# First gate and up blocks of the second feed-forward layer in alternating fours of halves, with all of x for them turned by VectorE

## The reference

```python
x = x + 0.5 * swiglu(rms_norm(x, n1), g1, u1, d1)          # D_FF = 5632
x = x + head_group_mixer(rms_norm(x, n2), w_in, ..., w_out) # 16 attention heads, 4 retention heads
x = x + 0.5 * swiglu(rms_norm(x, n3), g2, u2, d2)          # the layer that is changed
y = rms_norm(x, final)
def swiglu(h, w_gate, w_up, w_down):
    return (silu(h @ w_gate) * (h @ w_up)) @ w_down
```

## Time and profile before

| what | value |
|---|---|
| median of three runs | 1797.8 us (1797.42 to 1798.38) |
| the profiled execution, its own time | 1797.76 us |
| its span | 1795.9 us |
| TensorE matmul busy | 1786.4 us, 99% |
| VectorE busy | 1271.0 us, 71% |
| ScalarE busy | 811.8 us, 45% |
| mean granted TensorE clock | 0.999 of full |

### The profile page before, as it was taken

The page is one execution under the profiler, slowest core; times in us unless marked ns, Lnnn a source line. Parts: engine busy times, 40 slices in busy tenths (PEclk is TensorE's granted clock), DMA queues, the critical chain, the costliest instruction groups (busy, mean ns, idle before and its releaser), DMA issues.

```text
span 1795.9 us, 22263 instructions
## 1 busy us (share of the span) xinstructions
PE 1786.4 (99%) x8104; PEld 1476.3 (82%) x8104; DVE 1271.0 (71%) x1622; ACT 811.8 (45%) x976; POOL 59.2 (3%) x57
## 2 busy tenths in 40 slices
PE   9999999999999999999999999999999999999998
PEld 7888888888888888888888888888888888888886
DVE  6676676676676678688888786676676667667668
ACT  6434444444443444555455445443443443444444
POOL 0000000000000000002222000000000000000000
PEclk9999999999999999999999999999999999999999
DMA  9655565565555555555546456556556556655552
GB/s 382 206 187 190 198 195 187 190 199 195 187 191 199 193 187 193 182 168 190 183 163 211 141 181 217 193 199 193 187 192 200 192 187 192 200 192 187 193 200 97
DMA packets 175590, 346.66 MB, mean 193 GB/s; under 512 B 5952, under 2 KB 8640, under 8 KB 175424
## 3 DMA queue, kind: packets, MB, share of 16 engines
q1 hardware_dynamic: 174976, 345.35, 57.8%
q10 hardware_dynamic: 576, 0.81, 0.1%
HBM read 344.04 MB, written 2.10 MB: 193 GB/s over the span
## 4 chain that ended last, share of the span: by engine, by line
PE 98%; DMA 0%; ACT 0%; issue 0%; DVE 0%; SPq 0%; POOLq 0%; POOL 0%; DVEq 0%; ACTq 0%
PE ps L381 32%; PE ps L382 32%; PE ps L383 32%; PE ps L410 0%; DMA raw<-in_g 0%; PE ps L598 0%; PE ps L587 0%; PE ps L523 0%; PE ps L536 0%; ACT w_hi L656 0%; PE ps L487 0%; PE ps L486 0%; PE ps L485 0%; SPq L337 0%; ACT xT_hi L663 0%
## 5 line engine op out<-in xcount | busy, mean ns | idle before, releaser
L901 DVE TENSOR_TENSOR w_lo<-raw,w_hi 128x1024 fp32r<-128x1024 f32 x644 | 797.3, 1239 | 496.7 <-ACT w_hi L679 495.3
L679 ACT ACTIVATE w_hi<-raw 128x1024 fp32r<-128x1024 f32 x644 | 681.3, 1059 | 955.6 <-PE ps L383 948.8
L381 PE MATMUL ps<-w_hi,xT_hi 128*128 128x512 f32 (+1 forms) x1808 | 702.2, 388 | 0.3 <-DVE xT_lo L934 0.3
L382 PE MATMUL ps<-w_lo,xT_hi 128*128 128x512 f32 (+1 forms) x1808 | 700.2, 387 | 0.0
L383 PE MATMUL ps<-w_hi,xT_lo 128*128 128x512 f32 (+1 forms) x1808 | 700.0, 387 | 0.0
L381 PEld LDWEIGHTS ps<-w_hi,xT_hi 128*128 128x128 f32 x1808 | 339.5, 188 | 71.2 <-issue 1.4
L383 PEld LDWEIGHTS ps<-w_hi,xT_lo 128*128 128x128 f32 x1808 | 339.5, 188 | 69.6
L382 PEld LDWEIGHTS ps<-w_lo,xT_hi 128*128 128x128 f32 x1808 | 339.6, 188 | 68.5
L383 PE MATMUL ps<-w_hi,hT_lo 128*128 128x512 f32 x640 | 249.0, 389 | 0.0
L381 PE MATMUL ps<-w_hi,hT_hi 128*128 128x512 f32 x640 | 249.0, 389 | 0.0
L382 PE MATMUL ps<-w_lo,hT_hi 128*128 128x512 f32 x640 | 249.0, 389 | 0.0
(11 more groups left out here) (116 smaller groups left out, 540.0 us busy)
## 6 DMA issues: line engine op xcount, KB each, us to landing
raw<-in_u SPq DMA_DIRECT2D x88, 1024.0 KB, 5.1
raw<-in_d SPq DMA_DIRECT2D x88, 1024.0 KB, 4.9
raw<-in_g SPq DMA_DIRECT2D x85, 1024.0 KB, 5.1
raw<-in_w_in SPq DMA_DIRECT2D x40, 1024.0 KB, 4.9
raw<-in_w_out SPq DMA_DIRECT2D x16, 1024.0 KB, 5.0
raw<-in_g SPq DMA_DIRECT2D x4, 512.0 KB, 7.6
x<-in_x SPq DMA_DIRECT2D x4, 512.0 KB, 12.8
raw<-in_w_in SPq DMA_DIRECT2D x4, 512.0 KB, 3.7
```

Of the source, the lines that this page charges most:

```text
L381: pe.matmul(out, xh, wh, start=first and j == 0, stop=False)
L382: pe.matmul(out, xh, wl, start=False, stop=False)
L679: act.activation(w_hi[:, k % LEAD, :, 0:width], words[:, :, 0:width], ACT.Copy).then_inc(hi_ready, 1)
L901: dve.tensor_tensor(w_lo[:, k % LEAD, :, 0:width], words[:, :, 0:width], f32(w_hi[:, k % LEAD, :, 0:width]), ALU.subtract).then_inc(lo_rea ...
```

## The change

All four quarters of x are turned by VectorE for this layer. Quarter 1 takes the place of quarter 2 beside the output projection (`NEXT_X`, q = 26 to 31). Quarters 2 and 3 are turned in the layer itself, four block transposes behind each of positions 0 to 3 (`THIRD_X`) and 4 to 7 (`FOURTH_X`). Each pair gets a PSUM bank of its own number. TensorE's four calls of `turn_x` for this layer go.

The first gate and up blocks are mixed: positions 0 to 3 are gate with pairs 0 to 3, 4 to 7 up with pairs 0 to 3, 8 to 11 gate with pairs 4 to 7, and 12 to 15 up with pairs 4 to 7 (`first_both`). The loads of these two blocks follow that order. `xT` of pairs 2 and 3 moves ahead of position 0, of pairs 4 and 5 ahead of position 5, and of pairs 6 and 7 ahead of position 8. The first `silu` moves from position 9 to position 13, since the gate block is whole only after position 11.

```diff
-X_BY_DVE = [(FFN2, 0), (FFN2, 2)]
+X_BY_DVE = [(FFN2, 0), (FFN2, 1), (FFN2, 2), (FFN2, 3)]
-LATER_X = {28: (0, 2), 29: (2, 5), 30: (5, 9), 31: (9, 16)}
+NEXT_X = {26: (0, 3), 28: (3, 6), 29: (6, 9), 30: (9, 13), 31: (13, 16)}
+THIRD_X = {0: (0, 4), 1: (4, 8), 2: (8, 12), 3: (12, 16)}
+FOURTH_X = {4: (0, 4), 5: (4, 8), 6: (8, 12), 7: (12, 16)}
+FIRST_PARTS = {1: (4,), 2: (5,), 3: (6,), 4: (7,)}
+LATER_PARTS = {0: (2, 3), 5: (4, 5), 8: (6, 7)}
...
-            return (0, 1, 2, 3, 4, 5, 2, 3)[p]
+            return p if norm == FFN2 else (0, 1, 2, 3, 4, 5, 2, 3)[p]
...
+                        if f == 1 and isinstance(i, int):
+                            load(g + part, s, rows(ffn_w[f][s // 2], 4 * P * (2 * part + s % 2), i * W))
...
-                    if norm == FFN2 and bank == B_GATE and k in (2, 3):
-                        turn_x(norm, k + 4)
+            def first_both(g):
+                for pos in range(16):
+                    p, bank = 4 * (pos // 8) + pos % 4, (B_GATE, B_UP)[pos % 8 // 4]
+                    if bank == B_GATE:
+                        pe.wait_ge(xT_lo_ready, PAIRS * FFN2 + p + 1)
+                    half(g + pos // 8, pos % 8, xT_hi, xT_lo, 2 * p, bank, p == 0, p == 7)
...
-                if q == 26:
-                    for p in (2, 3):
-                        turn_x(FFN2, p)
...
-                    if 1 <= k < 5:
-                        xT((FFN1, FFN2)[f], k + 3)
+                    for p in (FIRST_PARTS, LATER_PARTS)[f].get(k, ()):
+                        xT((FFN1, FFN2)[f], p)
                     position(g0, k)
+                    if f == 1 and k in THIRD_X:
+                        turn_x(FFN2, 2, *THIRD_X[k])
+                    if f == 1 and k in FOURTH_X:
+                        turn_x(FFN2, 3, *FOURTH_X[k])
...
-                if q in (27, 29):
+                if q == 27:
                     for p in range(2):
-                        xT(FFN2, q - 27 + p)
+                        xT(FFN2, p)
```

More of the change, by code:

```diff
@@ L306, in load_ffn_in @@
                     for s in range(4):
-                        if 4 * part + s >= loaded:
+                        if f == 1 and isinstance(i, int):
+                            load(g + part, s, rows(ffn_w[f][s // 2], 4 * P * (2 * part + s % 2), i * W))
+                        elif 4 * part + s >= loaded:
                             load(g + part, s, rows(ffn_w[f][part], 4 * P * s, i * W))
@@ L424, in turn_x @@
                     pe.wait_ge(h_ready, T * NF)
-                elif (norm, p) == (FFN2, 2):
-                    pe.wait_ge(retT_lo_ready, RH)
-                    pe.wait_ge(y_raw_ready, T * RH)
                 for j in range(2):
@@ L440, in wide @@
                         continue
-                    if norm is not None and bank == B_GATE:
-                        pe.wait_ge(xT_lo_ready, PAIRS * norm + k + 1)
+                    if norm == FFN1 and bank == B_GATE:
+                        pe.wait_ge(xT_lo_ready, k + 1)
                     half(g, k, xT_hi, xT_lo, 2 * k, bank, k == 0, k == 7)
-                    if norm == FFN2 and bank == B_GATE and k in (2, 3):
-                        turn_x(norm, k + 4)
+            def first_both(g):
[4 more added lines that the diff above has]
+                    half(g + pos // 8, pos % 8, xT_hi, xT_lo, 2 * p, bank, p == 0, p == 7)
             def down(f, g, i):
@@ L490, in ffn @@
             def ffn(f):
-                norm = (FFN1, FFN2)[f]
-                wide(norm, G_FFN[f], B_GATE)
-                wide(norm, G_FFN[f] + 1, B_UP)
                 if f == 0:
+                    wide(FFN1, G_FFN[f], B_GATE)
+                    wide(FFN1, G_FFN[f] + 1, B_UP)
                     pe.wait_ge(ident_loaded, 16)
+                else:
+                    first_both(G_FFN[f])
                 def step(i):
@@ L715, in silu @@
             def silu(f, g, i):
-                act.wait_ge(half_used, 8 * g + 8)
+                act.wait_ge(half_used, 8 * g + (12 if f == 1 and isinstance(i, int) else 8))
                 for t in range(T):
@@ L732, in ffn @@
                 for k in range(16):
-                    if 1 <= k < 5:
-                        xT(norm, k + 3)
+                    for p in (FIRST_PARTS, LATER_PARTS)[f].get(k, ()):
+                        xT(norm, p)
                     position(g0, k)
@@ L739, in ffn @@
                         squares(norm, k - 4)
-                    if k == (13 if f == 0 else 9):
+                    if k == 13:
                         act.wait_ge(rstd_ready, (FFN1, FFN2)[f] + 1)
@@ L1244, in _ @@
                     turn_x(FFN2, 0, *FIRST_X[q])
-                if q in LATER_X:
-                    turn_x(FFN2, 2, *LATER_X[q])
-                if q in (27, 29):
+                if q in NEXT_X:
+                    turn_x(FFN2, 1, *NEXT_X[q])
+                if q == 27:
                     for p in range(2):
-                        xT(FFN2, q - 27 + p)
+                        xT(FFN2, p)
             ffn(1)
```

## The result

The changed kernel takes 1814.24 us (median of four runs, 1813.58 to 1814.59) against 1798.07 for the kernel before on the same runs: a ratio of 1.0091, with a 95% interval of 1.0079 to 1.0103. It is slower, as forecast, but by 16.2 us and not by 9.4, so the time lies 4.6 us above the range. The profiled execution took 1814.59 us.

The account below looks back on a forecast made before the run. TensorE was taken to bound the kernel. 1797.76 - 1.88 (transposes removed) + 9.7 (waits for VectorE) + 1.6 (lower clock) = 1807.2 us, 0.5% above; range 1804.9 to 1809.6 us.

Parts of the forecast that it names:

- The gain, 1.88 us: At the changed layer boundary TensorE loses 16 transposes, all on the path: 1.88 us saved.
- VectorE as the bound, 9.7 us late at position 10: VectorE's 32 added block transposes fall where it has no gap; TensorE's waits up to position 10 sum to 9.7 us.
- The walk: VectorE's program followed start to start up to pair 6: 9.7 us of TensorE waits, bounds 9.0 to 10.5.
- the three places: TensorE waits on xT_lo ahead of positions 2, 8 and 10: 3.0, 0.5 and 6.2 us.
- The wait of 0.5 us ahead of position 8: TensorE, 3.0 us late, reaches pair 4 at 1092.8; the pair is whole at 1093.3: 0.5 us.
- The clock, 1.6 us: TensorE's clock falls to half level in the wait ahead of position 10, costing 1.6 us, bounds nothing to 3.2.
- the wait of 3.0 us at position 2: Pair 2 is due at TensorE at 1073.5 but whole at 1076.5: a 3.0 us wait.
- Behind that nothing is late.: After position 10 no further wait; the first silu, at position 13, would cost at most 1.3 us if its cover were gone.
- A wait on w_lo that had not been seen: Named sign that the prediction is wrong: TensorE waiting on w_lo, for which the forecast held no time.
- VectorE keeps up: Rival: pairs 4 to 7 come in time at the changed boundary, the 1.88 us gain stands: 1795.9 us; chance 0.06.
- more comes of it: Rival: losses beyond the forecast waits and lower clock, 1809.6 us and above; chance 0.05.
- the two ways that were named: The lower clock lasts longer than at the start, or a late weight slot adds a wait behind position 10: 1809.6 and above.

Follow-up runs that it names:

- experiment 9: Experiment 1's kernel with quarter 1 turned by TensorE, VectorE's transposes respread, positions 8 to 15 in alternating twos, xT of pairs 6 and 7 later: 1797.05 us.
- experiment 1: The changed kernel with silu of the last step waiting for eight halves again, as before the change, not twelve: 1808.14 us.
- experiment 4: Experiment 1's kernel with 24 further matmuls, whose results nothing reads, between positions 9 and 10 on TensorE: 1806.77 us.
- experiment 8: Experiment 7's kernel with xT of pairs 6 and 7 one position later on ScalarE and VectorE: 1802.14 us.
- Experiment 2: The kernel before the change, with only silu of the last step of the second layer waiting for twelve halves, not eight: 1803.48 us.
- experiment 7: Experiment 1's kernel with positions 8 to 15 in alternating twos of gate and up, so pair 6 is wanted at position 12: 1804.02 us.
- Experiment 3: Experiment 1's kernel with quarter 3 of x turned by TensorE behind positions 5 and 6, not by VectorE: 1801.6 us.

## Why the prediction was wrong

**The gain, 1.88 us.** Not measured by itself for all 16 transposes; eight of them gave 0.93 in experiment 9, for 0.99 in the sum.

**VectorE as the bound, 9.7 us late at position 10.** Right in the mechanism. Position 2 was due at 1076.44 - 3.03 = 1073.41, so position 10, eight halves on, at 1095.2; it started at 1105.67, 10.5 us late: waits of 3.03 and 5.58, 1.7 of half clock in between, and 0.2 because the last matmul ahead of a wait is shown longer than the distance between starts. The walk was out by 0.8 us, at the upper edge of its bounds. VectorE's positions made most of that: the five from 1077.19 to `xT_lo` of pair 4 at 1092.85 took 3.13 us each, not 3.05. Of the three places two were right. The wait of 0.5 us ahead of position 8 did not come, because TensorE, slowed by the half clock, reached pair 4 only when it was whole.

**The clock, 1.6 us.** The mechanism was right at position 10, the size too small in the profiled execution: 5.29 - 2.72 = 2.6; by the medians of experiments 1 and 4 it is 1.4. I had not thought that the wait of 3.0 us at position 2 would be enough; it was. But its 1.7 us of half clock cost nothing of their own, since VectorE sets when pair 6 is whole: without them TensorE would have waited that much longer for pairs 4 and 6. That is argued, not shown in this kernel, but experiment 8 bears it out: its profiled execution kept the full clock, waited 0.69 + 1.23 us for these pairs, and is with 1802.75 us the longest of its eleven.

**"Behind that nothing is late."** This step failed. I looked at the first `silu` alone ("The first silu stands at position 13 on ScalarE, with two halves of TensorE to cover its 1.3 us") and did not ask where else its new condition is true. It is true in the last step, and costs 3.56 + (4.44 - 2.72) = 5.3 us there. Experiment 2 shows it alone, experiment 1 shows the rest without it: 1808.14, within the range. A wait on w_lo that had not been seen was among the signs of being wrong that the prediction named.

**The sum as it was:** 1797.76 - 1.88 + 10.5 + 2.6 + 5.3 = 1814.3, and the profiled execution took 1814.59. Without the late `silu`, and with the 1.4 us of the medians for the clock, it gives 1797.9 - 1.88 + 10.5 + 1.4 = 1807.9, where experiment 1 has 1808.14.

**The rivals.** That VectorE keeps up is refuted by the two waits on it at the changed place. That more comes of it happened, but mainly by neither of the two ways that were named: in the profiled execution the lower clock did last longer than at the start, but the 5.3 us of the late `silu` are more than that. The rule of the Trainium skill, "TensorE: Matmul & The Clock Gate", section "What's actually happening", that idleness brings the half rate back, agrees with these traces: 0.50 behind the waits of 3.03, 5.58 and 3.56 us, and 1.00 in experiment 4, where other matmuls filled the gap of 5.6. In experiment 8, though, the clock held behind 3.04 us.

## What to carry to other kernels

An engine that is 71% busy on the page can be full for 45 us where it matters: before giving it work, walk its program from its last idle gap to the moment at which the bounding engine wants the result, lateness at entry included. A later due time helps only by as much as the added work does not eat, and moves the wait to whatever stands behind it in an in-order program. Where a change touches a helper that several steps call, check its new condition at every call, the last one above all.

## What the runs showed of the hardware

Short waits were enough for the lower clock: 0.50 stood behind waits of 3.03 and 3.56 us, and it fell behind one of 2.20 in experiment 7, while at the end of the run before it took 4.9 us without a matmul, and behind the 3.04 us of experiment 8 it did not fall at all. Experiment 3, with a single such wait, has times in two groups: three from 1800.02 to 1800.72 with a mean granted clock of 0.999, and eight from 1801.55 to 1803.23 with 0.997 or 0.998. The medians of the groups lie 1.6 us apart. I read that as the price of one fall: the profiled execution, of the second group, has a clock of 0.50 from 1078 to 1080, behind its wait. For the first group it is not shown, since no trace has one of its executions. VectorE's block transposes cost the same with twice as many of them, a median of 457 ns against 456.
